# A two-layer trunk on one core: the even mixer written as one stream of projection steps, with the steps of its heads and groups placed in it

## The reference: what is computed

```python
q, k, v, g, a_low, z, xbc, dt = split(h @ w_in)
log_a = log_sigmoid(a_low @ w_gate2 + b_gate2) / 16          # 4 heads, dk 128, dv 256
o = gla_chunked(q, k, v, log_a)                              # causal, state decayed per key channel
o = rmsnorm(o, gla_norm_w) * silu(g)
xs, bm, cm = split(silu(causal_conv(xbc)))                   # 16 heads of 64 in 4 groups
dt = softplus(dt + dt_bias)
y = ssd_chunked(xs * dt, -exp(a_log) * dt, bm, cm) + d_skip * xs
y = rmsnorm(y * silu(z), by group) * ssm_norm_w
out = concat(o, y) @ w_out
```

## Time and profile before

| | us |
|---|---|
| median of 3 runs (lowest to highest) | 2365.56 (2363.37 to 2369.52) |
| the profiled execution | 2367.07 |
| its span in the trace | 2365.3 |
| the even mixer in the trace: from the first turn of its second token chunk (380.3) to that of the next sublayer's (990.5) | 610.2 |
| the SwiGLU block behind it, between the same marks | 364.2 |

### The profile page before, as it was taken

How to read it: one execution, slowest core, us unless ns; L and a number is a source line. 1 busy time by engine, 2 the same in 40 slices (tenths; PEclk the granted TensorE clock), 3 DMA queues, 4 the chain that set the end, 5 groups by cost and what they waited for, 6 DMA issues and landing times.

```text
span 2365.3 us, 25040 instructions
## 1 busy us (share of the span) xinstructions
PE 2239.2 (95%) x10358; PEld 1812.3 (77%) x10358; DVE 1009.8 (43%) x1438; ACT 739.3 (31%) x1141; POOL 193.0 (8%) x128
## 2 busy tenths in 40 slices
PE   7999999798888888999999999999998789999999
PEld 6888888677765666888888888888886348888887
DVE  4333224458876665443332343332265335333322
ACT  4222223433333333332221232222233434322211
POOL 0000001332212120000000000000033000000000
PEclk9999999899998889999999999999999779999999
DMA  5332332221111112242323232323222002332331
GB/s 180 95 102 89 107 98 71 79 71 45 54 36 37 43 36 101 69 134 89 107 89 107 72 125 92 104 89 107 90 83 75 15 0 71 118 106 89 107 98 54
DMA packets 55298, 197.31 MB, mean 83 GB/s; under 512 B 6272, under 2 KB 6784, under 8 KB 55184
## 3 DMA queue, kind: packets, MB, share of 16 engines
q1 hardware_dynamic: 53856, 193.75, 25.4%
q10 hardware_dynamic: 1328, 1.96, 0.2%
HBM read 193.58 MB, written 2.10 MB: 83 GB/s over the span
## 4 chain that ended last, share of the span: by engine, by line
PE 61%; DVE 4%; issue 3%; ACT 2%; POOL 1%; DVEq 0%; ACTq 0%; POOLq 0%
PE ps L789 11%; PE ps L790 11%; PE ps L791 11%; PE ps L797 7%; PE ps L799 7%; PE ps L798 7%; PE ps L1162 1%; PE ps L1161 1%; DVE a_rows L1226 1%; ACT a_rows L415 1%; ACT a_rows L727 1%; DVE a_rows L1223 1%; DVE temps L1223 1%; PE ps L1042 0%; PE ps L1172 0%
## 5 line engine op out<-in xcount | busy, mean ns | idle before, releaser
L789 PE MATMUL ps<-h_hi,w_hi 128*128 128x512 f32 (+1 forms) x1976 | 746.8, 378 | 12.4 <-DVE temps L1599 9.2
L791 PE MATMUL ps<-h_hi,w_lo 128*128 128x512 f32 (+1 forms) x1976 | 734.4, 372 | 0.0
L790 PE MATMUL ps<-h_lo,w_hi 128*128 128x512 f32 (+1 forms) x1976 | 733.9, 371 | 0.0
L415 ACT ACTIVATE w_hi<-raw 128x1024 fp32r<-128x1024 f32 x352 | 370.5, 1056 | 790.5 <-PE ps L799 392.4
L1223 DVE TENSOR_TENSOR w_lo<-raw,w_hi 128x1024 fp32r<-128x1024 f32 x288 | 343.7, 1221 | 338.0 <-ACT w_hi L415 337.4
L789 PEld LDWEIGHTS ps<-h_hi,w_hi 128*128 128x128 f32 x1976 | 376.4, 190 | 86.1 <-issue 21.1
L791 PEld LDWEIGHTS ps<-h_hi,w_lo 128*128 128x128 f32 x1976 | 376.2, 190 | 64.3
L790 PEld LDWEIGHTS ps<-h_lo,w_hi 128*128 128x128 f32 x1976 | 376.6, 191 | 61.8 <-issue 2.5
L1223 DVE TENSOR_TENSOR a_rows<-a_rows,ps 128x512 f32<-128x512 f32 x88 | 60.5, 688 | 614.0 <-PE ps L791 614.0
L797 PE MATMUL ps<-w_hi,a_hi 128*128 128x512 f32 x704 | 274.4, 390 | 0.0
L799 PE MATMUL ps<-w_hi,a_lo 128*128 128x512 f32 x704 | 274.0, 389 | 0.0
(11 more groups left out here) (182 smaller groups left out, 1918.9 us busy)
## 6 DMA issues: line engine op xcount, KB each, us to landing
raw<-in_w_gate_up SPq DMA_DIRECT2D x176, 512.0 KB, 3.7
raw<-in_w_down SPq DMA_DIRECT2D x88, 512.0 KB, 3.5
raw<-in_w_xbc SPq DMA_DIRECT2D x16, 512.0 KB, 3.5
raw<-in_w_zg SPq DMA_DIRECT2D x16, 512.0 KB, 3.5
raw<-in_w_even_out SPq DMA_DIRECT2D x16, 512.0 KB, 3.6
raw<-in_w_qk_small SPq DMA_DIRECT2D x9, 512.0 KB, 3.5
raw<-in_w_v SPq DMA_DIRECT2D x8, 512.0 KB, 3.5
raw<-in_w_odd_out SPq DMA_DIRECT2D x8, 512.0 KB, 3.5
```

Source lines behind the costliest of these rows:

```text
L415: return nc.scalar.activation(to, source, ACT.Copy, scale=scale)
L789: nc.tensor.matmul(to, w_h, hi, start=first, stop=False)
L790: nc.tensor.matmul(to, w_h, lo, start=False, stop=False)
L791: return nc.tensor.matmul(to, w_l, hi, start=False, stop=last)
```

## The change

Everything of the even mixer is written anew; the sublayers around it keep their code, but for one input of `out_stage` (where it starts).

- **One stream.** The slots come as q/k/small (9), v and g of heads 0, 1 and then of 2, 3 (16), conv inputs of group 0 (4), z of groups 0, 1 (4), conv of groups 1, 2 (8), z of group 2 (2), conv of group 3 (4), z of group 3 (2), output (16): 65 again. On PE a generator, `projections`, gives one block of three passes at a time, up to the first half of the output projection, and `project_to(place)` advances it. `plan_even` gives every step of heads and groups a place in blocks: head `h` starts at 12 + 41h with levels 3 to 5 blocks apart, group `g` at 176 + 45g.
- **Who makes what.** q, k, v, silu(g) and silu(z) leave PSUM by ACT (the last two by silu at once), and the conv reads PSUM itself, on ACT and DVE, without a copy. v, g, z are held with tokens on the partitions, and so are the heads' and groups' outputs.
- **Norms.** The squares are summed by ACT's accumulator over a token's row, so PE's sums and spreads and DVE's diagonals go; the head's output is scaled and gated by DVE, turned back by 8 transposes, and its high part (ACT, `cat_high`) and low part (DVE, `cat_low`) go from PSUM straight to `cat`.
- **Groups.** The difference of the log decays is one matmul of K = 32 per chunk (`source_rows` x `head_rows`), so the DVE step is one instruction (min with 0) per head instead of four; the skip term is a matmul with a diagonal; x and far blocks are 256 columns wide.
- **Order.** ACT and DVE have `keep_up(place)`, which takes whatever tile, block or z has its last block before that place. The step sizes (`dt`) are done with 64 rows, on DVE inside head 0. z of groups 2 and 3 is made by matmuls of 256 columns, 96 for a pair of slots.
- **GpSimd** makes the low parts of 51 slots instead of 49, in program order with the eight powers; DVE's share begins behind them. The loads of the next gains are put 7 slots later or more.

```diff
+def plan_even():
+    at = {}
+    for h in range(GH):
+        base = 12 + 41 * h
+        for j, step in enumerate((0, 3, 7, 10, 14, 17, 22)):
+            at["level", h, j] = base + step
+        at["own", h], at["far", h], at["out", h], at["head_turn", h] = base + 25, base + 30, base + 36, base + 61
+    for g in range(SG):
+        base = 12 + 41 * GH + 45 * g
+        for name, step in (("x", 0), ("cb", 10), ("skip", 20), ("y_far", 35), ("group_turn", 49)):
+            at[name, g] = base + step
+        for r in range(4):
+            at["decay", g, r] = base + (13, 16, 22, 27)[r]
+            at["near", g, r] = base + (22, 27, 31, 35)[r]
+    tile_end = [128 + 8 * (n + 1) + (32 if n >= 4 else 0) + (16 if n >= 12 else 0) for n in range(16)]
...
@@ gpsimd
-                    split_some("qk_small", INNER, 9)
-                    split_some("v", 0, 8)
-                    split_some("xbc", 0, INNER)
...
+                    n = first_slot[EVEN] + 4
+                    places = [even_at["out", h] + 4 for h in range(GH)] + [even_at["near", g, 3] + 6 for g in range(SG)]
+                    for norm, place in enumerate(places):
+                        while n < min(stream + place // 8 + 4, INNER_END):
+                            split_low(n)
+                            n += 1
+                        power(norm)
...
@@ scalar
+                def split_to(place):
+                    while upcoming["slot"] < min(stream + place // 8 + 4, INNER_END):
+                        split_high(upcoming["slot"])
+                        upcoming["slot"] += 1
+                def keep_up(place):
+                    conv_to(place)
+                    take_z(place)
+                    for g in range(SG):
+                        if tile_end[4 * g + 1] + 5 <= place:
+                            silu_x(g)
+                        if tile_end[4 * g + 3] + 5 <= place:
+                            silu_bc(g)
+                    split_to(place)
+                def head(h):
...
+                    for j in range(len(SPANS)):
+                        take_blocks(even_at["level", h, j])
+                        decay_of(j)
+                        keep_up(even_at["level", h, j])
+                        if j == 5 and h:
+                            turn_head(h - 1)
...
@@ tensor
+                def projections():
+                    for n in range(4, 9):
+                        if n == 8:
+                            pe.wait_ge(tile_taken, QK0 + 4)
+                        yield from tile(first_slot[s] + n, first_bank(n))
+                    pe.wait_ge(tile_taken, QK0 + 8)
+                    for b in range(4):
+                        yield from token_tiles(stream + 4 * b, lambda c: pe.wait_ge(vg_taken, 4 * (b - 1) + c + 1) if b else None)
+                    for n in range(4):
+                        pe.wait_ge(vg_taken, 12 + n + 1)
+                        yield from tile(stream + 16 + n, n)
...
+                    yield from first_half(s, block_source, lambda index: pe.wait_ge(cat_lo_ready, index + 1))
+                def project_to(place):
+                    while placed[0] < place:
+                        next(projecting)
+                        placed[0] += 1
+                def head(h):
                     for j in range(len(SPANS)):
+                        project_to(even_at["level", h, j])
+                        if j == 6 and h:
+                            turn_head(h - 1)
                         pe.wait_ge(gla_factors, h * 8 + (j + 1))
...
-                        project(2)
@@ vector
+                        if j == 5 and h:
+                            dve.wait_ge(vg_taken, 8 if h < 3 else 16)
+                            gate()
+                        if j < len(SPANS):
+                            keep_up(even_at["level", h, j])
+                        if j == 2 and h + 1 < GH:
+                            log_decay(h + 1)
+                        if j == 3 and h == 0:
+                            step_sizes()
+                        if j == 5 and h == 1:
+                            far_step_sizes()
```

More of the change, by code:

```diff
@@ new lines, in take_blocks @@
+                def take_blocks(place):
+                    while upcoming["block"] < 4 and 32 * (upcoming["block"] + 1) <= place:
+                        b = upcoming["block"]
+                        act.wait_ge(slot_done, stream + 4 * b + 4)
+                        for c in range(NC):
+                            if b % 2 == 0:
+                                copy(rows(a_rows, V_ROWS + 2 * b + c), ps[:, c, :]).then_inc(vg_taken, 1)
+                            else:
+                                nc.scalar.activation(rows(a_rows, G_ROWS + 2 * (b - 1) + c), ps[:, c, :], ACT.Silu).then_inc(vg_taken, 1)
+                        upcoming["block"] += 1
@@ L922, in even @@
                 s = EVEN
-                first_four(s)
-                projection("qk_small", 4, 6)
-                pe.wait_ge(even_in, 48)
-                pe.wait_ge(tile_taken, QK0 + 4)
-                for h in range(GH):
-                    last = nc.tensor.matmul(ps[:, 4 + h, :], gate2[:, h * P:h * P + P], small[0:RANK, :], start=True, stop=True)
-                last.then_inc(decay_logits, 1)
-                projection("qk_small", 6, 9)
-                first = stages["v"][0]
-                for half in range(2):
+                q, k = [[rows(a_rows, row + h) for h in range(GH)] for row in (Q, K)]
@@ L1086, in odd @@
+                for g in range(SG):
+                    group(g)
+                project_to(even_at["group_turn", SG - 1])
+                turn_group(SG - 1)
+                for _ in projecting:
+                    pass
+                second_half(s, block_source)
             def odd():
@@ L1406, in even @@
[L1406 to L1415 removed]
+                first = first_slot[EVEN]
@@ L1668, in ssm_groups @@
-                    gate(0)
-                    outputs(1)
-                    dve.wait_ge(y_gated, g * 2 + 1)
-                    take(2)
-                    gate(1)
-                    dve.wait_ge(group_squares, g + 1)
-                    tt(square_sum, square_sum, other[0], ALU.add).then_inc(group_summed, 1)
-                    norm(g + norms[("ssm", 0)], 256, head_rstd)
-                    for m in range(2):
-                        row = rows(a_rows, g * 2 + (XS + m))
-                        last = stt(row, row, mixer_cols[:, ds(g * 2 + (94 + m), 1)], head_rstd, ALU.mult, ALU.mult)
@@ L1680, in ssm_groups @@
[L1680 to L1687 removed]
+                    keep_up(even_at["near", g, 3])
+                    pair = token_pair.rearrange("p (c v) -> p c v", c=2)
+                    dve.wait_ge(y_far_done, g + 1)
```

1171 lines of the change are left out of this document (650 added, 521 removed).

## The result

The changed kernel takes **2406.4 us** (median of 4 runs, 2405.3 to 2411.0) against 2366.4 before: a ratio of 1.0173, 95% interval 1.0154 to 1.0192. It is 40 us slower where 16 us less were forecast, and outside the range.

The account below looks back on a forecast made before the run. PE was taken to bound the kernel, the even mixer losing time to waits and slow clock. Floor 488.7, idle 75.8, small losses 6 and clock 24 made 594.5 us, 15.7 less than 610.2, hence 2350 in all; range 2325 to 2358.

Parts of the forecast that it names:

- the floor's first term: PE in the even mixer: 65 slots of 24 passes, one every 0.227 us, take 353.6 us.
- the losses stay as they are: Rival for the even mixer: waits change places, the clock costs 40 as before; 2368 us in all, chance 0.13.
- floor 488.7: PE's work in the changed even mixer without losses: 486.2 plus 2.5 us for the edits.
- hidden 6: Even mixer: unshown small losses, taken as 6 us.
- idle PE: Even mixer: PE's waits in about 30 chains of helper-engine steps, 75.8 us in sum against 72 before.
- the clock: Even mixer: PE slowed after a dozen waits of 2.5 us or more, 2 us each, 24 us against 40 before.
- The waits at a head's first level: From head to head: squares (taken as 2.3), weight copy, exp, two factors against 5 blocks; 2.2 us, three times.
- a turn before level 6: Turn of a head: transposes, two high copies, exp and factors against 3 blocks; 2.6 us, three times.
- head 3's levels: Three conv taps in a row, and ACT's first tap, ahead of factors: waits of 3.2, 3.9 and 4.6 us.
- the end of group 0: Conv tile, table load, silu and weight copy, then the scaled copies: a wait of 4.8 us.
- The slower rival: Even mixer: GpSimd's splits hold up DVE's factors, 1.7 us a hit; 2381 us with half the chains hit, chance 0.29.
- The fast rival: Even mixer: half the chains hide, stage 541 us, 69 less; 2296 us in all, chance 0.20.

Follow-up runs that it names:

- e5: Changed kernel with mixer_cols 196 columns wide instead of 172, tensors at multiples of 128 bytes again: 2359.8 us.
- e2: Kernel before with mixer_cols 140 columns wide instead of 132, tensors 32 bytes past a multiple of 64: 2409.3 us.
- e9: e5 with a head's turn copies behind level 6's exp, squares behind the next head's first factors, head 3's taps one or two at a time: 2335.4 us.
- e10: e9 with step sizes in four pieces, the last conv tile ahead of group 2's squares, the mean ahead of DVE's taps: 2322.9 us.
- e11: e10 with ACT's weight copies in the heads directly behind a level's exp instead of ahead of it: 2315.8 us.
- e6: Kernel before with mixer_cols 148 columns wide instead of 132, h and a_rows at an odd multiple of 64 bytes: 2394.2 us.
- e8: Kernel before with 64 bytes of padding between h_lo and a_rows, only a_rows and what follows moved: 2386.1 us.
- e1: Changed kernel with mixer_cols 180 columns wide instead of 172, tensors at odd multiples of 64 bytes: 2389.7 us.
- e3: Changed kernel with 32 bytes of padding between h_lo and a_rows, h still 32 bytes off, a_rows at a multiple of 64: 2396.0 us.

## Why the prediction was wrong, and where it was right

**The step that failed** is the floor's first term. "A 512-column pass starts every 0.227 us" was read in the kernel before and carried over to the changed one for all 352 slots, together with "nothing is to be had there" on the SwiGLU blocks. The pass is no constant of the matmul's shape: with its operands 32 bytes further on it took 0.233 to 0.234. None of the rivals had it either, though the width of `mixer_cols` stood in the diff. It is worth 57 us by passes; from e5 to the change it measures 46.6, and on the kernel before (e2) 44. What is missing lies mostly in the mixers: the even mixer's 65 slots would take 10.5 us more by passes, and it took 4.0 (604.5 against 600.5).

**With that taken out** the forecast is tested by e5: 2359.8 us, where 2350 was said and 2325 to 2358 was the forecast's own range, so it is 10 us short. The sign holds at the measurement's edge. That is also the lower edge of the rival "the losses stay as they are" (2368, give or take 8). Term by term, PE's busy time of 533.2 us being split by the clock records:

| term of the mixer | forecast | e5 |
|---|---|---|
| work at full clock: floor 488.7 and hidden 6 | 494.7 | 497.2 (533.2 less half of 72.0) |
| idle PE | 75.8 | 67.3 (600.5 less 533.2) |
| clock | 24 | 36.0 (half of the 72.0 us busy at 0.50) |
| mixer | 594.5 | 600.5 |

So the second term that was mis-sized is **the clock**: 24 us for "a dozen waits" at 2 us each, against 36.0. In the kernel before the same reckoning gives 38.1, near the 40 that was taken. The mean grant is 0.93 in the change as against 0.92 before, where 0.94 or more was to be seen. The waits of 2 us and more are 16 in e5's mixer and 14 before; so there were not fewer of them, and the clock's cost stayed. Where waits were taken out it fell: PE was busy at 0.50 for 61.7 us in e9, 45.3 in e10 and 34.1 in e11.

The sum of the idle time came out near, partly by luck: single terms missed in both directions. The waits at a head's first level were given as 2.2 each and are 2.23, three times; the step sizes 5.5, measured 3.9; the start 4.7, measured 2.9; a turn before level 6 2.6, measured 3.7, three times; head 3's levels 3.2, 3.9 and 4.6, measured 4.2, 5.3 and 6.0; behind group 2 6.3, measured 5.1; the gate of the last head 3.5, measured 2.5; the own blocks 0.9, four times, measured none; the end of group 0 4.8, measured 2.3. ACT there, in the changed kernel:

```profile
770.74 0.42 ACT L763 ACTIVATE junk<-early_rows 128x256 uint8<-128x256 f32 x1 [7.37 <-DVE late_rows L1462]
...
772.36 0.76 ACT L640 ACTIVATE a_rows<-ps,mixer_cols 128x512 f32<-128x512 f32 x1
773.14 1.28 ACT L649 ACT_TABLE_LOAD   x1
774.43 1.06 ACT L649 ACTIVATE a_rows<-a_rows 128x1024 f32<-128x1024 f32 x1
775.39 1.04 ACT L479 ACTIVATE w_hi<-raw 128x1024 fp32r<-128x1024 f32 x1
779.98 0.91 ACT L479 ACTIVATE early_rows<-early_rows,rstd_col 128x256 f32<-128x256 f32 x2 [3.54 <-POOL rstd_col L430]
```

The four squares take 1.6 us (770.74 to 772.36), less than the 2.3 taken. The silu starts 0.01 us behind its table load, and then ACT stands idle for 3.5 us: the scaled copies wait for the mean, which DVE takes behind its conv taps, and the power, not for the table. So in these rows a load costs its 1.28 and no more, and here it was not on the path.

**The slower rival** (0.29) named GpSimd's splits. It is not why the kernel is slower. In e5 a factor of 256 columns takes 600 ns on average against 417 before, which is 10 us of DVE over 56 of them: seven take 0.8 to 2.3 us, and none did before. Of the differences five take 1.4 to 2.6 us, and before it was four with 2.6. That is fewer than the 13 more hits from which the rival made the change slower. e10 and e11 show the collision real: 2.15 us at each of two levels. Whether all of the 7 us between the two runs is its doing is not shown, since e11's edit moves the 1.04 us copies themselves too, in all heads. The fast rival (half the chains hide) did not come: DVE was busy 263.9 of e5's 600.5 us, and the chains of single steps still did not hide.

## What to carry to other kernels

Before the time of an edit is judged, compare the start addresses of the operands in the two programs: where untouched stages change their pace at a full clock, look whether the layout moved, and try first to pad a small tensor so that the matmul operands start again where they did, here at odd multiples of 128 bytes. Where many short waits remain in a stream with engines half idle, the order on the helper engines is the lever: what the next matmul needs goes ahead of what merely has to be done, and a GpSimd step with two SBUF inputs is started just behind, not just ahead of, DVE's step on the path. The kernel that results here (e11) has the rewritten mixer, tensors at multiples of 128 bytes and seven steps moved or divided, and takes 2.15% less than the kernel before, where the change as made takes 1.7% more.

## What the runs showed of the hardware that was not expected

A 512-column fp32r pass takes 0.2267 us with both operands at odd multiples of 128 bytes. It takes 0.2289 to 0.2343 on average with one of them 32 or 64 bytes off. This holds for the moving operand (gate and up passes of e6, 0.2289) and for the stationary one (down passes of e8, 0.2333, with the moving weights in place). At 64 bytes it is 0.2289 or 0.2333: gate and up 0.2289 in e6 and 0.2333 in e1, down 0.2333 in e6 and e8 and 0.2289 in e1 and e3. What exactly is paid off 128 stays open. Even multiples of 128, and two operands that are off by the same amount, were not tried.
